# Token blocks of 96 slots in place of 128 in the expert stage of a two-layer decoder kernel

## The reference

```python
def _swiglu(h, w_gate, w_up, w_down):
    return (jax.nn.silu(h @ w_gate) * (h @ w_up)) @ w_down

def _moe(h, w_router, w_gate, w_up, w_down):
    t = h.reshape(b * s_len, d)                       # 256 x 1024
    logits = (t @ w_router).astype(jnp.float32)       # 8 experts
    top_val, top_idx = lax.top_k(logits, TOP_K)       # TOP_K = 2
    weights = jax.nn.softmax(top_val, axis=-1)
    gates = jnp.sum(jax.nn.one_hot(top_idx, N_EXPERTS) * weights[..., None], axis=1)
    for e in range(N_EXPERTS):
        y = y + gates[:, e:e + 1] * _swiglu(t, w_gate[e], w_up[e], w_down[e])
```

## Time and profile before

| | |
|---|---|
| median of three runs | 1439.76 us (1439.07 to 1440.60) |
| span of the profiled execution | 1441.4 us |
| TensorE busy | 1411.7 us, 98% |
| weight loads busy | 1190.6 us, 83% |
| VectorE / ScalarE busy | 1204.6 us (84%) / 1015.5 us (70%) |
| chain that ended last | PE 92%, DVE 6%, ACT 1% |
| moved by DMA | 435.24 MB, mean 302 GB/s |

### The profile page before, as it was taken

The page is one execution under the profiler, slowest core; times in us unless marked ns, Lnnn a source line. Parts: engine busy times, 40 slices in busy tenths (PEclk is TensorE's granted clock), DMA queues, the critical chain, the costliest instruction groups (busy, mean ns, idle before and its releaser), DMA issues.

```text
span 1441.4 us, 18581 instructions
## 1 busy us (share of the span) xinstructions
PE 1411.7 (98%) x7176; PEld 1190.6 (83%) x7176; DVE 1204.6 (84%) x1299; ACT 1015.5 (70%) x1239; POOL 76.9 (5%) x87
## 2 busy tenths in 40 slices
PE   7999999999999999999999999999999999999997
PEld 6787999988788888888888888888888888888885
DVE  6976555557976899999999999998999999999996
ACT  4664544444764688878888888888888888888884
POOL 0210000000210100000000010010000001000000
PEclk9999999999999999999999999999999999999999
DMA  8633952253624999999999999999999999999970
GB/s 281 220 116 132 351 178 78 95 183 118 218 75 181 399 394 391 368 395 389 370 382 387 372 374 390 367 370 393 390 371 383 386 375 367 392 378 367 394 279 31
DMA packets 187404, 435.24 MB, mean 302 GB/s; under 512 B 7887, under 2 KB 14773, under 8 KB 187317
## 3 DMA queue, kind: packets, MB, share of 16 engines
q1 hardware_dynamic: 183748, 421.93, 79.0%
q0 software_dynamic: 3136, 10.54, 2.5%
q10 hardware_dynamic: 432, 1.57, 0.3%
HBM read 426.66 MB, written 7.37 MB: 301 GB/s over the span
## 4 chain that ended last, share of the span: by engine, by line
PE 92%; DVE 6%; ACT 1%; issue 0%; DMA 0%; SPq 0%; POOL 0%; POOLq 0%; ACTq 0%; DVEq 0%
PE ps L1743 84%; PE ps L2099 2%; DVE split L1469 2%; PE ps L1868 1%; PE ps L1833 1%; DVE E L1278 1%; PE ps L1849 1%; DVE E L1296 1%; DVE neg_max L1281 1%; PE ps L2061 0%; PE ps L1940 0%; PE ps L1734 0%; DMA x<-in_x 0%; PE ps L2072 0%; PE ps L2042 0%
## 5 line engine op out<-in xcount | busy, mean ns | idle before, releaser
L1743 PE MATMUL ps<-split,hTs 128*128 128x512 f32 (+2 forms) x3456 | 801.1, 389 | 2.3 <-DVE split L1469 1.2
L1743 PEld LDWEIGHTS ps<-split,hTs 128*128 128x128 f32 x3456 | 637.0, 188 | 130.5 <-issue 5.3
L1469 DVE TENSOR_TENSOR split<-ring_a,split 128x1024 fp32r<-128x1024 f32 (+2 forms) x480 | 573.8, 1214 | 98.8 <-ACT split L1035 36.4
L1046 ACT ACTIVATE split<-ring_a 128x1024 fp32r<-128x1024 f32 x384 | 406.1, 1061 | 98.3 <-PE ps L1743 98.1
L1469 DVE TENSOR_TENSOR split<-ring_b,split 128x1024 fp32r<-128x1024 f32 x322 | 388.5, 1223 | 69.4 <-ACT split L1035 35.7
L1743 PE MATMUL ps<-split,acts 128*128 128x512 f32 x1584 | 373.9, 392 | 0.0
L1046 ACT ACTIVATE split<-ring_b 128x1024 fp32r<-128x1024 f32 x288 | 304.6, 1063 | 74.8 <-PE ps L1743 74.0
L1743 PEld LDWEIGHTS ps<-split,acts 128*128 128x128 f32 x1584 | 296.6, 188 | 63.9
L1743 PE MATMUL ps<-hTs,split 128*128 128x256 f32 x1056 | 128.3, 283 | 0.8 <-DVE hTs L1469 0.8
L1743 PEld LDWEIGHTS ps<-hTs,split 128*128 128x128 f32 x1056 | 127.5, 190 | 1.7 <-DVE hTs L1469 1.3
L918 ACT ACTIVATE split<-ring_a 128x1024 fp32r<-128x1024 f32 (+2 forms) x64 | 60.3, 977 | 13.3 <-PE ps L1743 7.8
(11 more groups left out here) (197 smaller groups left out, 609.7 us busy)
## 6 DMA issues: line engine op xcount, KB each, us to landing
ring_a<-in_w_exp_gate SPq DMA_DIRECT2D x32, 2048.0 KB, 11.2
ring_a<-in_w_exp_up SPq DMA_DIRECT2D x32, 2048.0 KB, 11.7
ring_a<-in_w_exp_down SPq DMA_DIRECT2D x32, 2048.0 KB, 11.6
ring_b<-in_w_exp_gate SPq DMA_DIRECT2D x24, 2048.0 KB, 9.7
ring_b<-in_w_exp_up SPq DMA_DIRECT2D x24, 2048.0 KB, 10.6
ring_b<-in_w_exp_down SPq DMA_DIRECT2D x24, 2048.0 KB, 10.6
ring_a<-in_w_in SPq DMA_DIRECT2D x8, 2048.0 KB, 8.8
ring_a<-in_w_out SPq DMA_DIRECT2D x4, 2048.0 KB, 11.0
```

The lines of the kernel that those rows point to most:

```text
L1046: act.activation(ex_unit(v)[0], ex_part(c, u), ACT.Copy).then_inc(hi_done, 1)
L1469: dve.tensor_tensor(dst, src, high.bitcast(F32), ALU.subtract).then_inc(signal, 1)
L1743: ins = pe.matmul(dst, a[ia], b[ib], start=(first and i == 0), stop=(last and i == 2))
```

## The change

`SLOTS` becomes 96, and with it `ROUNDS` 3. A block holds 96 token rows: the stationary operand of the gate, up and down matmuls has 96 columns in place of 128, their outputs 96 partitions; gathers and scatters move 96 rows; the transposes read 96 rows against an identity of 96 x 96. The number of matmuls, of moving columns in `product` and `down`, of weight loads and of bytes of weights is the same. After the first round each engine has two branches, one for each further round. The buffers keep their spacing of 128.

```diff
-SLOTS = 128
+SLOTS = 96
 ROUNDS = -(-SEQ // SLOTS)
...
-        ex_actTs = [acts[:, :, b * FW:(b + 1) * FW].rearrange("p i (q n) -> p i q n", q=4) for b in range(2)]
-        ex_act = [ff_act[:, b * FW:(b + 1) * FW] for b in range(2)]
-        xg = hn[:, 0, :]
-        ex_out = hn[:, 1, :]
+        ex_actTs = [acts[:, :, b * FW:(b + 1) * FW].rearrange("p i (q n) -> p i q n", q=4)[:, :, :, 0:SLOTS]
+                     for b in range(2)]
+        ex_act = [ff_act[0:SLOTS, b * FW:(b + 1) * FW] for b in range(2)]
+        xg = hn[0:SLOTS, 0, :]
+        ex_out = hn[0:SLOTS, 1, :]
...
+        def turned_act(n):
+            return ps[:, 4 + n % 2, :].rearrange("p (q n) -> p q n", q=4)[:, :, 0:SLOTS]
...
-                pool.wait_ge(xy_again, 16 * TILES)
-                pool.wait_ge(stored, 16 * TILES)
+                pool.wait_ge(xy_again, 16 * TILES * r)
+                pool.wait_ge(stored, 16 * TILES * r)
...
-                act.activation(ex_act[n % 2], ps[:, 0, :], ACT.Silu).then_inc(silu_done, 1)
+                act.activation(ex_act[n % 2], ps[0:SLOTS, 0, :], ACT.Silu).then_inc(silu_done, 1)
...
-                dve.tensor_scalar(sel[:, t, :], cst("iota1"), place[:, t, 0:1], None, ALU.is_equal).then_inc(sel_done, 1)
+                dve.tensor_scalar(sel[:, t, 0:SLOTS], cst("iota1")[:, 0:SLOTS], place[:, t, 0:1], None, ALU.is_equal).then_inc(sel_done, 1)
...
-                        ins = pe.matmul(xg_bank()[:, c, :], hn[:, t, c * P:(c + 1) * P], sel[:, t, :],
+                        ins = pe.matmul(xg_bank()[:, c, :], hn[:, t, c * P:(c + 1) * P], sel[:, t, 0:SLOTS],
...
-                    ins = pe.transpose(xg_bank()[:, c, :], xg[:, c * P:(c + 1) * P], ident)
+                    ins = pe.transpose(xg_bank()[:, c, :], xg[:, c * P:(c + 1) * P], ident[0:SLOTS, 0:SLOTS])
...
-                        ins = three(ps[:, bank, :], [xgTs[i % 2][:, h, 2 * u + k, :] for h in range(2)],
+                        ins = three(ps[0:SLOTS, bank, :], [xgTs[i % 2][:, h, 2 * u + k, :] for h in range(2)],
...
-                    ins = pe.transpose(ps[:, 4 + n % 2, q * P:(q + 1) * P], ex_act[n % 2][:, q * P:(q + 1) * P], ident)
+                    ins = pe.transpose(turned_act(n)[:, q, :], ex_act[n % 2][:, q * P:(q + 1) * P], ident[0:SLOTS, 0:SLOTS])
...
-                        ins = three(ps[:, 2 + h, :], [ex_actTs[n % 2][:, p, q, :] for p in range(2)],
+                        ins = three(ps[0:SLOTS, 2 + h, :], [ex_actTs[n % 2][:, p, q, :] for p in range(2)],
```

More of the change, by code:

```diff
@@ L387, in build @@
         g_row = sb("g_row", [P, D_MODEL])
-        sumsq = sb("sumsq", [P, 6, TILES])
-        rstd = sb("rstd", [P, 6, TILES])
+        sumsq = sb("sumsq", [P, 2 * DEPTH + ROUNDS, TILES])
+        rstd = sb("rstd", [P, 2 * DEPTH + ROUNDS, TILES])
         half_neg = sb("half_neg", [P, 16])
@@ L440, in build @@
         facts = sb("facts", [P, 2, TILES, 3], U32)
-        sel = sb("sel", [P, TILES, SLOTS])
+        sel = sb("sel", [P, TILES, P])
         back_id = sb("back_id", [P, 1 + TILES])
-        xgTs = [hTs[:, :, :, :].rearrange("p i c n -> p (i c n)")[:, b * 2 * KC * SLOTS:(b + 1) * 2 * KC * SLOTS].rearrange(
-            "p (i c n) -> p i c n", i=2, c=KC) for b in range(2)]
+        xgTs = [hTs[:, :, :, :].rearrange("p i c n -> p (i c n)")[:, b * 2 * KC * P:(b + 1) * 2 * KC * P].rearrange(
+            "p (i c n) -> p i c n", i=2, c=KC)[:, :, :, 0:SLOTS] for b in range(2)]
         last_acts = sb("last_acts", [P, 2, FW], F32R)
@@ L865, in _ @@
                     for r in range(ROUNDS):
[L866 to L867 removed]
+                        pool.dma_start(slots_d.rearrange("(r p e) k -> r p (e k)", r=ROUNDS, p=SLOTS)[r],
+                                       empty_i[0:SLOTS, :]).then_inc(empty_out, 16)
             token_rows()
@@ L1114, in put_out @@
                     act.wait_ge(meta_in, 16 * ROUNDS)
-                    if i == LAST_ITEM + 1:
-                        act.wait_ge(stored, 16 * TILES)
+                    if i and i % EXPERTS == 0:
+                        act.wait_ge(stored, 16 * TILES * (i // EXPERTS))
                     elif scatters_before(i):
                         act.wait_ge(scattered, 16 * scatters_before(i))
-                act.activation(ex_out[:, xcols(h)], ps[:, 2 + h, :], ACT.Copy, scale=gate_of(i)).then_inc(eo_done, 1)
+                act.activation(ex_out[:, xcols(h)], ps[0:SLOTS, 2 + h, :], ACT.Copy, scale=gate_of(i)).then_inc(eo_done, 1)
             def expert_items(first):
@@ L1585, in back_rows @@
                 dve.wait_ge(meta_in, 16 * ROUNDS)
-                link(dve.tensor_copy(back_id[:, 0:1], meta[:, 0, LAST_ITEM, 1:2]))
+                link(dve.tensor_copy(back_id[0:SLOTS, 0:1], meta[0:SLOTS, 0, LAST_ITEM, 1:2]))
                 for t in range(TILES):
-                    ins = dve.tensor_scalar(back_id[:, t + 1:t + 2], back_id[:, 0:1], float(1 - P * t), None, ALU.add)
+                    ins = dve.tensor_scalar(back_id[0:SLOTS, t + 1:t + 2], back_id[0:SLOTS, 0:1], float(1 - P * t), None, ALU.add)
                 link(ins)
                 for t in range(TILES):
-                    dve.tensor_scalar(sel[:, t, :], cst("iota1"), back_id[:, t + 1:t + 2], None,
+                    dve.tensor_scalar(sel[0:SLOTS, t, :], cst("iota1")[0:SLOTS, :], back_id[0:SLOTS, t + 1:t + 2], None,
                                       ALU.is_equal).then_inc(back_done, 1)
@@ L2145, in add_last @@
                     for h in range(2):
-                        pe.matmul(ps[:, 4 * t + h, :], sel[:, t, :], ex_out[:, xcols(h)],
+                        pe.matmul(ps[:, 4 * t + h, :], sel[0:SLOTS, t, :], ex_out[:, xcols(h)],
                                   start=True, stop=True).then_inc(back_ps, 1)
```

22 lines of the change are left out of this document (11 added, 11 removed).

## The result

The changed kernel takes 1443.58 us (median of 13 runs, 1442.49 to 1445.13), the kernel before 1440.6 us in the 13 runs taken beside them. The ratio is 1.0021 with a 95% interval of 1.0013 to 1.0028: 3.0 us slower, where 4.1 us faster was forecast. The time lies inside the range given (1418 to 1444), but its sign is the other one.

The account below looks back on a forecast made before the run. TensorE's unbroken stream was taken to bound the expert stage. Transposes -7.5 us and the end's jump +3.4, all else zero, gave 4.1 us off the 1439.8 us median: 1435.7 us, range 1418 to 1444 (0.80).

Parts of the forecast that it names:

- these 4032 matmuls: Expert matmuls of line 1743, 512 moving columns, 228.3 ns each: narrowing the stationary operand to 96 columns changes nothing.
- transposes: 280 transposes on lines 2099 and 2072: 96 moving columns save 26.7 ns each, 7.5 us in all.
- end: Program end: a second far jump over a skipped round, on VectorE, adds 3.4 us, bounds 0.5 and 4.0.
- The bounds I gave: For the 4032 expert matmuls: at best 60 us gained, at worst the weight load lies bare, +121 us.
- the sign turns at 1 ns per matmul: Expert matmuls: a loss above 1 ns each, 4.1 us in all, decides against the forecast gain.
- Rival 1: Expert matmuls: the 96-column load lies bare, 30 ns more each, +121 us, 1557 us; chance 0.12.
- Rival 2: Expert matmuls: the 15 ns excess shrinks with stationary columns, giving 1420.6 us, or 1385 to 1395 if hidden; chance 0.15.
- Rival 3: Transposes keep 109 ns each, so only the end's jump is left: 1443.2 us, 0.24% slower; chance 0.07.
- Rival 4: An expert with more than 96 tokens makes a further round run, some 950 us; chance 0.02.
- The first tokens: 16 matmuls on line 2061 with `sel` as moving operand, now 96 columns: no change, at best 1.6 us.
- all work off the path: VectorE and ScalarE steps, gathers, scatters, table of places: no gain, as TensorE waits for none of them.
- three tests that I had named: Wrong if 72 matmuls leave 16.3 to 16.6 us, four transposes still take 0.44, or VectorE's drain comes within 5 us.

Follow-up runs that it names:

- e7: The kernel before with only a gap of 96 bytes ahead of the hidden values (`acts`); 1445.95 us, ratio 1.0041.
- e2: The kernel before with only the gate, up and down matmuls at 96 stationary columns; 1451.93 us, ratio 1.0085.
- e3: The changed kernel with two rounds of 96 in place of three, buffers back at their earlier addresses; 1445.6 us, ratio 1.004 to the kernel before.
- e9: The changed kernel with two rounds, expert tokens and hidden values placed at distance 144 bytes from the moving operand; 1428.22 us, ratio 0.9911 to the kernel before.
- s1: The kernel before with 128 down to 32 stationary columns in its eight items; only paces read, tokens 226.8 to 233.3 ns.
- e1: The kernel before with only the 280 transposes narrowed to 96 moving columns; 1435.9 us, ratio 0.997.
- e10: The kernel before with code and branch of a third round of 128 that never runs, `acts` kept in place modulo 256 bytes; 1443.01 us, ratio 1.0015.
- e4: The changed kernel with the third round's branch inside the second's, so skipping both takes one jump; 1442.11 us, ratio 1.0016 to the kernel before.
- s2: The kernel before, 128 columns, stationary operands moved 16 bytes further per item, 128 more in odd items or steps; tokens 226.8 to 234.3 ns.
- s3: The kernel before with 96 stationary columns, operands moved 16 bytes further per item, 128 more in odd items or steps; tokens 226.7 to 231.7 ns.
- e6: The changed kernel with two rounds, expert tokens and hidden values placed at distance 16 bytes from the moving operand; 1453.96 us, ratio 1.0094 to the kernel before.
- s4: The kernel before with moving operand `split` 16 bytes further in a longer buffer, which moves the stationary operands by 128; 1465.63 us.
- s5: The s2 kernel with `split` and the stationary operands all moved by 128 bytes; only paces read, tokens 226.7 to 234.3 ns.
- e12: The kernel before with 64 unused bytes ahead of the hidden values (`acts`); 1436.36 us, ratio 0.998.
- e11: The whole change with three rounds, its operands placed at the distances of e9; 1433.14 us, ratio 0.9948 to the kernel before.

## Why the prediction was wrong

**The step that failed** is "I therefore put these 4032 matmuls at no change". In the changed kernel the products take 0.65 us more per item, 5.2 us in all, and the same kind of matmul in the dense part 1.1 us more. Against the forecast's -7.5 + 3.4 = -4.1 us the terms came out as transposes -6.2 (8 x 0.77), products +5.2, dense part +1.1 and end +3.0, together +3.1. Two errors are in the step.

First, the pair of rows that carried it, float32 transposes with 96 and 128 stationary columns, both 0.60 us, can't tell. Those instructions take about 109 ns by their 128 moving columns, and the effect that was found, 0 to 8 ns on fp32r matmuls that stand at 227 ns, is outside of what they sample. The bounds I gave were honest (0 gained to the bare load), but the point in them was taken from the wrong kind of instruction.

Second, the change moves a buffer, and no term of the sum was for that. ROUNDS goes from 2 to 3, three tables grow, and `acts` moves by 96 bytes, from distance 192 to 32. The whole diff shows it, but neither the part of it shown above nor the order of the instructions; that the buffers keep their spacing, as I had written, is true and says nothing of where they start. Alone, at 128 columns, the shift takes 228.9 ns to 233.4 and costs 5.9 us (e7), about as much as any term that I had. At 96 columns it happens to go the other way, 233.4 (e2, e3) to 228.9. So the hidden values of the experts came out unchanged by two effects that cancel, and the dense ones, at 128 columns, took the loss.

The term was small per matmul: the experts lost 1.3 ns of 229. The prediction had said that the sign turns at 1 ns per matmul, and it turned there.

**The rivals.** Rival 1 had the direction and the threshold, and a false mechanism: no load lies bare. The loads are shorter (161 ns mean in the item, before 188 in the earlier trace rows), and e9 runs 96 columns at 226.8 ns. Its price was off as well: it takes 0.47 ns a column from float32 loads, and the fp32r loads of s1 grow by 0.84 (134 ns with 64 columns, 188 with 128). The rule of the Trainium skill that went with it ("TensorE: Matmul & The Clock Gate", section "Weight-path perf modes") is not seen at work in any run here: 128 and 96 columns reach the same 226.7 ns, and the hidden values of s1 have no step at 128. Rival 2 is false as well: s1 goes down to 32 columns, and no pace falls below 226.7; what stands above 213.3 ns doesn't shrink with the load's width. Rival 3 gave 1443.2 us, nearly the measured 1443.58, and its mechanism is false: the transposes did speed up. A time that fits is no evidence for the story behind it. Rival 4: no further round ran.

**What was right.** The transposes: 0.33 and 0.66 us, exactly. Their yield was 0.77 us per item in the changed kernel and 0.74 alone (e1), where 0.94 was forecast: the matmuls behind a turn give a little back. The end: +3.0 us for +3.4, set by VectorE's second jump (e10, e4); SyncE's second one was longer than its first, 2.5 us in place of 0.5, and stays just covered; the forecast, which gave it 0.5 for its short code, had this wrong without harm. The first tokens and all work off the path: nothing, under an unbroken TensorE stream. None of the three tests that I had named as making me wrong struck (72 matmuls within 16.3 to 16.6 us, four transposes at 0.33, a drain 7.0 us behind the branch): the first was drawn too wide for its purpose, since 0.1 us in it is 5.6 us in the kernel.

**Open.** Why the place of one operand against the other counts, and what decides beside the distance modulo 256 bytes: within one item of s1 (112 columns, one distance) groups of 48 take 11.23 and 11.44 us in turn, s2 and s3 have two paces at distances 144 and 176, and s3 and e6 differ at 16. The values are 226.7 ns at best, which is 544 cycles of 2.4 GHz for 512 columns, and 233.3, which is 560, with others between; the 256-column matmuls take 120.0, 288 cycles. So there are 32 cycles in each that no experiment removed.

## What to carry to other kernels

When TensorE sets the time, look up how far its stationary and moving operands start from each other, modulo 256 bytes, before and after any edit, even one that only grows a table in front of them; then try a gap, which takes no time of its own, and measure it: the distance alone doesn't foretell the pace in every layout. Price a matmul by rows of its own type and pace, and ask of every "no change" what it costs per instruction times their number. A block that is never executed still costs its jump at the end of the program, on each engine that can be last.

## What was not expected of the hardware

- The pace of fp32r matmuls with 512 moving columns depends on where the operands lie: 226.7 to 234.3 ns at 128 stationary columns (s2), 226.7 to 233.4 at 96 (s3, e2, e6), and up to 234.7 with the moving operand shifted (s4).
- It is the place of one operand against the other: both moved by 128 bytes change nothing (s5), one of them changes 6.5 ns (e6, e9), and `acts` moved by 256 bytes changes nothing (e10). The best distance differs with the width: 0 at 128 columns (226.8 ns; 230.0 for 96), 144 at 96 columns (226.8; mostly 233.3 for 128). It isn't the whole rule: at 16 and 96 columns there are 233.3 ns (e6) and 226.7 (s3).
- At some distances a kernel has two paces by turns, 226.7 and 233.3 ns in groups of the same item (s2 at 144, s3 at 176).
- Within a kernel a shift of 96 unused bytes was worth 5.9 us (e7), and one of 64 bytes -2.9 us (e12).
- A jump over a skipped round (in e4 over two), from the branch to the engine's next instruction, takes 3.1 to 4.2 us on VectorE, 3.4 to 5.2 on TensorE and 2.6 to 4.8 on ScalarE (before, after, e4, e10, e11), and 0.2 on GpSimd. On SyncE it takes 0.5 us for the first round, and 2.2 to 2.5 for the third behind it (after, e10, e11).
